# A two-layer decoder trunk on one core: projections of unnormed tokens, with the norm weights in the weight splits and the token factors at the results

## The chip, the cores and the metric

The kernel runs on one core of a Trainium2 chip. The metric is device time in microseconds (us), from one launch of the whole program; lower is better. It was run three times.

## The reference, cut to what matters

Two layers work on x, 512 tokens of 1024 values, in fp32. Each layer has a mixer, a cross attention into 256 memory tokens and a mixture of experts (MoE); each sub-layer is fed by an RMS norm with its own weight vector.

```python
def rms_norm(x, g):
    y = x * rsqrt(mean(x * x, axis=-1, keepdims=True) + EPS)
    return y * g

for layer in range(2):
    h = rms_norm(x, norm_mix[layer])
    x = x + (fox_rglru_mixer(h, ...) if layer % 2 == 0 else spatial_gating_mixer(h, ...))
    x = x + memory_cross_attention(rms_norm(x, norm_cross[layer]), rms_norm(mem, norm_mem[layer]), ...)
    x = x + hierarchical_moe(rms_norm(x, norm_ffn[layer]), ...)

# fox_rglru_mixer:       q, k, v, f_logit, xb, gb = split(h @ w_in); forgetting attention on q, k, v;
#                        a gated linear recurrence on xb with gate gelu(gb); concat, @ w_out
# spatial_gating_mixer:  u, v = split(gelu(h @ w_in + b_in)); v = rms_norm(v);
#                        mixed = causal 128x128 position mixing of v per group + b_s; (u * mixed) @ w_out
# memory_cross_attention: q = rms_norm(h @ wq); k, v = split(mem_n @ wkv); k = rms_norm(k); softmax; @ wo
```

A projection of normed tokens, h @ w, is r * (x @ (g * w)), with one factor r for each token and one weight g for each row of w. The norms of q and k inside a projection's result hardly feel r at all: only their EPS does.

## The kernel before

All engines run one program written by hand, in five instruction streams that meet in semaphores. Work stands in each stream in a fixed order, and an engine that waits holds up everything behind it.

**Dense projections.** Every fp32 product is made of three products of rounded parts (fp32r): weight high by activation high (`wh`, `ah`), weight low by activation high (`wl`, `ah`), weight high by activation low (`wh`, `al`). A weight matrix is cut into chunks of 512 columns (`("in", l, c)`, `("cin", l, c)`, `("cout", l, c)`, `("kv", l, c)`, `("xq", l, c)` and so on), a chunk into steps of 128 rows (8, or 16 for `cout`). For each step ScalarE (ACT) rounds 128x512 weights from the ring into `wh` (`split_hi`, L524), VectorE (DVE) makes the rest `wl` (`split_lo`, L533), and TensorE (PE) issues 12 products (L657, or L654 where the result is wanted transposed, `flip`), 6 where the rows are the 256 memory tokens. `wh` and `wl` have three places (STAGE = 3), so a split waits until PE has used the step three before. `between={k: work}` puts other work into a stream ahead of step k; `lead` makes the first three steps go token tile by token tile, so that they can begin before all four tiles are there; `split_next` makes the first three splits of the next chunk.

**Results.** PSUM's eight banks are two halves of four. Each chunk, turn or small product is a "round" on one half; `begin` on PE waits until every earlier round on that half has been reported by `took` on DVE or ACT. `HALF` and `names` in `round_plan` say which half and in which order. After `begin` a chunk fills the half.

**Norms.** For each of the kinds mix, cross and mem: ACT squares and sums a tile of tokens (`tile_square`, L1344), GpSimd (POOL) adds EPS and takes the power -1/2 (`norm_power`, L2447, L2448), DVE writes x * r * g into a buffer `nat` (`scale`, L1791), PE turns it into PSUM with 8 transposes of 128x128 (`norm_T`, L700), ACT rounds it (`tile_hi`, L1361), DVE makes the rest (`tile_lo`, L1812). The weight rows g come in broadcast loads of 512 KB (`load_gain`).

**Order of the stages.** Layer 0: norm; chunks in 0 to in 4 (q, k, xb, v, gb) with the forget logits `thin_f` (L719) ahead of step 3 of in 0, the turns of q and k, and the maxima products (`tops`) between the steps of in 3 and in 4; two gate products (L876); scores and values (L843 to L858); out 0, out 1. Layer 1: norm; cin 0 to 3 (v), cin 4 to 7 (u), cout 0 with the spatial products (L910) between its steps, cout 1. In both: the turns of the memory tokens, kv 0 to 2, the turns of the cross tokens, xq 0, xq 1, kv 3, attention, xo, routing, then 16 pairs of experts. Some filler products keep PE at work while it would wait: `idle_turns` (L689) and `idle_products` (L683). At the end of a MoE the last pair is added by `last_adds` on DVE (L2330).

## Time and profile before

| | |
|---|---|
| median of 3 runs | 1936.49 us (1935.87 to 1937.17) |
| the profiled execution, its own time | 1935.72 us |
| its span, from the first to the last instruction | 1934.0 us |
| PE busy | 1888.2 us, 98% |
| DVE, ACT, POOL busy | 41%, 28%, 5% |
| mean granted clock of TensorE | 0.996 |

The profiled execution is one more run; its span leaves 1.7 us around it. "Busy" of PE counts the filler products too, and a pipelined matmul's end is modelled, so 98% is not 98% useful work. The granted clock is a share of full speed: 1.00 is 2.4 GHz, 0.50 is 1.2 GHz. A wait in a row of the timeline stands in brackets, with the instruction that ended it.

### The profile page before, as it was taken

Reading aid. Unit: us, or ns where it says so; the run is one execution under the profiler, and the core shown is the slowest. Engines: PE = TensorE matmul, PEld = TensorE weight load, DVE = VectorE, ACT = ScalarE, POOL = GpSimd, SP = SyncE. Lnnn points to the kernel's source line nnn. Section 1 sums busy time; section 2 is a strip of 40 time slices with the busy share of each in tenths; the row PEclk is TensorE's granted clock in tenths of the full one; section 3 lists DMA queues with packets and bytes.
Section 4 is the critical chain, followed back from the end, with each engine's and each line's share of the span. In section 5 each row is a group of like instructions: output and inputs, shape, how many; then the busy total and the mean of one; then the engine's idle time right before and its main releaser. Section 6 shows DMA issues by size and latency. Waiting matters only on the chain.

```text
span 1934.0 us, 22569 instructions
## 1 busy us (share of the span) xinstructions
PE 1888.2 (98%) x9316; PEld 1198.4 (62%) x9316; DVE 786.9 (41%) x1184; ACT 543.8 (28%) x1008; POOL 94.7 (5%) x121
## 2 busy tenths in 40 slices
PE   8999999999999999999999999999999999999998
PEld 7875777676444544444588887777674444544443
DVE  4465565535222322223433356455371322323223
ACT  4426353533111111111344333335351111111110
POOL 2200010000000000000100022000000000000000
PEclk9999999999999999999999999999999999999999
DMA  6210342135999999999733312332138999999997
GB/s 242 88 66 22 110 152 87 44 112 197 406 420 415 421 418 418 419 416 423 275 104 118 107 64 87 114 127 87 47 131 363 418 416 420 421 418 420 421 415 288
DMA packets 96409, 490.06 MB, mean 253 GB/s; under 512 B 7824, under 2 KB 7888, under 8 KB 47024
## 3 DMA queue, kind: packets, MB, share of 16 engines
q1 hardware_dynamic: 93552, 479.75, 62.5%
q0 software_dynamic: 2176, 7.76, 1.2%
q8 instruction: 78, 1.28, 0.3%
q10 hardware_dynamic: 576, 1.05, 0.1%
q14 instruction: 27, 0.22, 0.0%
HBM read 486.44 MB, written 2.10 MB: 253 GB/s over the span
## 4 chain that ended last, share of the span: by engine, by line
PE 86%; DVE 6%; ACT 4%; DMA 2%; issue 2%; POOL 1%; SPq 0%; POOLq 0%; DVEq 0%; ACTq 0%
PE ps L657 24%; PE ps L1064 22%; PE ps L1088 11%; PE ps L1029 6%; PE ps L654 6%; PE ps L1050 5%; PE ps L981 1%; ACT wh L524 1%; PE ps L700 1%; PE ps L858 1%; PE ps L962 1%; DVE wl L533 1%; PE ps L1043 1%; DMA ring<-in_moe_w_down 1%; DMA ring<-in_c_w_in 1%
## 5 line engine op out<-in xcount | busy, mean ns | idle before, releaser
L533 DVE TENSOR_TENSOR wl<-ring,wh 128x512 fp32r<-128x512 f32 x280 | 199.9, 724 | 334.7 <-ACT wh L524 333.5
L524 ACT ACTIVATE wh<-ring 128x512 fp32r<-128x512 f32 x280 | 174.1, 629 | 366.2 <-PE ps L657 285.5
L1064 PE MATMUL ps<-ring,xg 128*64 128x512 f32 x1248 | 276.0, 594 | 0.3
L657 PE MATMUL ps<-wh,ah 128*128 128x512 f32 x544 | 215.8, 397 | 4.9 <-issue 2.3
L657 PE MATMUL ps<-wh,al 128*128 128x512 f32 x544 | 212.1, 390 | 0.0
L657 PE MATMUL ps<-wl,ah 128*128 128x512 f32 x544 | 211.8, 389 | 0.0
L2260 DVE SCALAR_TENSOR_TENSOR hh<-ps,wcol,sg 128x512 f32<-128x512 f32 x32 | 36.9, 1152 | 387.9 <-PE ps L1064 387.9
L1064 PEld LDWEIGHTS ps<-ring,xg 128*64 128x64 f32 x1248 | 87.7, 137 | 172.7 <-issue 171.9
L2281 DVE TENSOR_TENSOR x<-ps,x 128x1024 f32<-128x1024 f32 x120 | 144.1, 1222 | 87.7 <-PE ps L1050 83.9
L1064 PE MATMUL ps<-slot,xg 128*64 128x512 f32 x800 | 177.8, 594 | 0.0
L1667 ACT ACTIVATE xg<-ps,grow 128x256 f32<-128x256 f32 x128 | 53.6, 471 | 283.2 <-PE ps L1029 264.6
L1088 PE MATMUL ps<-ring,hT 128*64 128x512 f32 x576 | 128.6, 595 | 0.0
L1064 PEld LDWEIGHTS ps<-slot,xg 128*64 128x64 f32 x800 | 56.3, 137 | 111.2 <-issue 111.2
L1029 PE MATMUL ps<-oh,xnh 128*128 128x256 f32 x480 | 122.2, 293 | 0.0
L657 PEld LDWEIGHTS ps<-wh,ah 128*128 128x128 f32 x544 | 102.2, 188 | 28.8 <-issue 3.3
L1029 PEld LDWEIGHTS ps<-oh,xnh 128*128 128x128 f32 x480 | 90.1, 188 | 47.1 <-issue 47.1
L2278 DVE TENSOR_TENSOR yl<-ps,yh 128x512 fp32r<-128x512 f32 x64 | 41.4, 686 | 185.9 <-ACT yh L1650 185.9
L1029 PE MATMUL ps<-oh,xnl 128*128 128x256 f32 x480 | 116.2, 281 | 0.0
L657 PEld LDWEIGHTS ps<-wh,al 128*128 128x128 f32 x544 | 102.1, 188 | 21.7
L657 PEld LDWEIGHTS ps<-wl,ah 128*128 128x128 f32 x544 | 102.2, 188 | 20.7 <-issue 0.5
L1650 ACT ACTIVATE yh<-ps 128x512 fp32r<-128x512 f32 x64 | 35.0, 596 | 254.7 <-PE ps L1088 246.5
L1050 PE MATMUL ps<-yh,selT 128*128 128x512 f32 x240 | 97.5, 406 | 0.0
(312 smaller groups left out, 2622.2 us busy)
## 6 DMA issues: line engine op xcount, KB each, us to landing
ring<-in_moe_w_gate SPq DMA_DIRECT2D x80, 1024.0 KB, 10.2
ring<-in_moe_w_up SPq DMA_DIRECT2D x76, 1024.0 KB, 10.9
ring<-in_moe_w_down SPq DMA_DIRECT2D x76, 1024.0 KB, 9.2
slot<-in_moe_w_up SPq DMA_DIRECT2D x52, 1024.0 KB, 10.1
slot<-in_moe_w_down SPq DMA_DIRECT2D x52, 1024.0 KB, 9.4
slot<-in_moe_w_gate SPq DMA_DIRECT2D x48, 1024.0 KB, 10.6
ring<-in_x_wkv SPq DMA_DIRECT2D x16, 1024.0 KB, 5.0
ring<-in_c_w_in SPq DMA_DIRECT2D x16, 1024.0 KB, 5.4
```

The costliest lines, as they stand in the source:

```text
L524: act.activation(wh[:, t % STAGE, :], ring[:, SLOT[unit], 512 * s:512 * (s + 1)], ACT.Copy).then_inc(wh_ready, 1)
L533: dve.tensor_tensor(wl[:, t % STAGE, :], ring[:, SLOT[unit], 512 * s:512 * (s + 1)], wh[:, t % STAGE, :].bitcast(F32), ALU.subtract).then_ ...
L654: mm = pe.matmul(ps[:, b + m, 0:T], w[:, (t0 + k) % STAGE, m * P:(m + 1) * P], a[:, k, :], **flags)
L657: mm = pe.matmul(ps[:, b + m, :], a[:, (k + k0) % steps, m * P:(m + 1) * P], w[:, (t0 + k) % STAGE, :], **flags)
L1029: mm = pe.matmul(ps[:, bank, kk * 256:(kk + 1) * 256], a[:, m, k * P:(k + 1) * P], oh[:, b % 2, m, :], start=(m == 0 and i == 0), stop=(m ...
L1050: mm = pe.matmul(ps[:, bank + half, :], selT[:, q % 2, m * P:(m + 1) * P], a[:, 512 * half:512 * (half + 1)], start=(i == 0), stop=(i == 1))
L1064: mm = pe.matmul(ps[p * SLOTS:(p + 1) * SLOTS, bank, :], xg[:, b % 2, k, r * P + p * SLOTS:r * P + (p + 1) * SLOTS], w(p)[:, k % 4, :], st ...
L1088: mm = pe.matmul(ps[p * SLOTS:(p + 1) * SLOTS, Y + half, :], hT[:, k, p * SLOTS:(p + 1) * SLOTS], w(p)[:, k % 2, 512 * half:512 * (half + 1)],
L1667: ins = act.activation(xg[:, b % 2, k, :], ps[:, bank, kk * 256:(kk + 1) * 256], ACT.Copy, scale=grow[:, l, k:k + 1])
L2260: return dve.scalar_tensor_tensor(out=hh[:, :].rearrange("p (k c) -> p k c", k=KF), in0=by_row(ps[:, UP, :]), scalar=wcol[:, 0:1], in1=by_ ...
L2278: return dve.tensor_tensor(yl[:, part], ps[:, Y + half, :], yh[:, part].bitcast(F32), ALU.subtract)
L2281: return dve.tensor_tensor(x[:, m, :], ps[:, bank:bank + 2, :].rearrange("p a n -> p (a n)"), x[:, m, :], ALU.add)
```

## The change

Tokens are no longer multiplied by r and g before they are turned. PE turns x and mem themselves; `nat`, its scales and the broadcast loads of g go. Three small loads on ACT's queue bring all g of the kinds mix, cross and mem, PE turns them once, and DVE copies them to `gcols`, a column of 128 for each step. The splits of in, cin, kv and xq take that column as a scale: ACT's copy has a scale operand, and DVE's subtraction becomes multiply and subtract (`scalar_tensor_tensor`). The factor r is applied where each result leaves PSUM: as a column where tokens are rows, and as a row over all partitions, `rrow`, where they are columns. PE makes `rrow` with four products of a broadcast column with the identity (`norm_row`), once in `thin_f` and once ahead of step 7 of cin 3, as a round of its own. The EPS of the q and k norms is scaled by the variance (`epsn`).

Work that moves with it:
- the squares of the mix norm go from before the turns into in 0 and cin 0 (ahead of ACT's splits 4, 5 and 6);
- `thin_f` goes from step 3 to step 6 of in 0, `f_inputs`, `f_terms` and `f_sums` go into in 1, ahead of its steps 1, 2 and 3;
- xb goes from an ACT copy to four DVE multiplies behind kTr in `k_out`, and the second k copy goes from DVE to ACT;
- gb and u are multiplied by `rrow` on DVE and then put through Gelu on ACT, from SBUF instead of PSUM; the last four multiplies of u stand between the first four `gated` steps;
- the cross tokens' turns 0, 1 and 2 go into kv 1 and kv 2, their high and low parts with them; turn 3 into the lead of xq 0;
- the memory tokens' turns of layer 1 go from step 14 of cout 0 to step 6 of cout 1;
- the first weight unit of in 0 is loaded right behind the first tile of x; the turns of the mix tokens of layer 0 go into the lead of in 0;
- the banks of the last mixes and of the turns change, so that the first two turns of layer 1 can begin while the last adds run.

```diff
-LAST_MIX = ((6, 7, 0, 1), (2, 5, 3, 4))
+LAST_MIX = ((6, 7, 5, 1), (2, 4, 3, 0))
...
-            names += [("cin", l, c) for c in range(4)] + [("cin", l, c) for c in range(4, 8)]
-            names += [("mix", l, 0), ("cout", l, 0)] + [("nmem", l, m) for m in range(MM)] + [("cout", l, 1)]
-            half.update({("mix", l, 0): 0, ("cout", l, 0): 1, ("nmem", l, 0): 0, ("nmem", l, 1): 0, ("cout", l, 1): 0})
-        names += [("kv", l, c) for c in range(3)]
-        names += [("ncross", l, m) for m in range(TM)] + [("xq", l, 0), ("xkT", l, 0), ("xkT", l, 1), ("xq", l, 1)]
+            names += [("cin", l, c) for c in range(4)] + [("rrow", l, 0)] + [("cin", l, c) for c in range(4, 8)]
+            names += [("mix", l, 0), ("cout", l, 0), ("cout", l, 1)] + [("nmem", l, m) for m in range(MM)]
+            half.update({("rrow", l, 0): 0, ("cin", l, 4): 0})
+            half.update({("mix", l, 0): 0, ("cout", l, 0): 1, ("nmem", l, 0): 1, ("nmem", l, 1): 1, ("cout", l, 1): 0})
+        names += [("kv", l, 0), ("ncross", l, 0), ("kv", l, 1), ("ncross", l, 1), ("kv", l, 2), ("ncross", l, 2), ("ncross", l, 3)]
+        names += [("xq", l, 0), ("xkT", l, 0), ("xkT", l, 1), ("xq", l, 1)]
         names += [("kv", l, 3)]
         half.update({("nmix", l, m): l for m in range(TM)})
-        half.update({("ncross", l, m): 1 for m in range(TM)})
+        half.update({("ncross", l, m): 0 if m == 1 else 1 for m in range(TM)})
...
+                g = gain_of_step(t)
                 if s == 0:
                     act.wait_ge(ring_full[SLOT[unit]], 16 * NTH_LOAD[unit])
                 after(act, w_used, t - STAGE + 1)
                 act.activation(wh[:, t % STAGE, :], ring[:, SLOT[unit], 512 * s:512 * (s + 1)],
-                               ACT.Copy).then_inc(wh_ready, 1)
+                               ACT.Copy, **({} if g is None else dict(scale=g))).then_inc(wh_ready, 1)
...
-                dve.tensor_tensor(wl[:, t % STAGE, :], ring[:, SLOT[unit], 512 * s:512 * (s + 1)],
-                                  wh[:, t % STAGE, :].bitcast(F32), ALU.subtract).then_inc(wl_ready, 1)
+                g = gain_of_step(t)
+                if g is None:
+                    dve.tensor_tensor(wl[:, t % STAGE, :], ring[:, SLOT[unit], 512 * s:512 * (s + 1)],
+                                      wh[:, t % STAGE, :].bitcast(F32), ALU.subtract).then_inc(wl_ready, 1)
+                else:
+                    dve.scalar_tensor_tensor(out=wl[:, t % STAGE, :], in0=ring[:, SLOT[unit], 512 * s:512 * (s + 1)], scalar=g,
+                                             in1=wh[:, t % STAGE, :].bitcast(F32), op0=ALU.mult, op1=ALU.subtract)\
+                       .then_inc(wl_ready, 1)
             return max(pos, upto)
...
-                    sp.wait_ge(nat_ready, nats_upto("cross", l))
+                    sp.wait_ge(S["rec_ready"], 4)
                 elif SLOT[unit] == RING + 3:
                     sp.wait_ge(S["half_squares"], 2 * TM * (l + 1))
                     sp.wait_ge(S["small_lo"], l + 2)
...
                     after(pe, taken[HALF[name]], NTH[name] - (1 if kind == "ncross" or m else 0))
                     b = first_bank(name)
-                    nats[0] += 1
-                    pe.wait_ge(nat_ready, nats[0])
+                    src = mem if kind == "nmem" else x
                     for k in range(KD):
+                        if k == 0 and kind == "nmem":
+                            pe.wait_ge(S["mem_loaded"], 16 * (l + 1))
+                        if k == 0 and kind == "ncross":
+                            pe.wait_ge(res_added, TM * 2 * l + m + 1)
+                        if k == 0 and kind == "nmix" and l == 0:
+                            pe.wait_ge(x_loaded[m], 16)
+                        if k == 0 and kind == "nmix" and l and m == 0:
+                            pe.wait_ge(S["half_out"], TM * (l - 1) + 2)
+                        if k == (0 if m else KD // 2) and kind == "nmix" and l:
+                            pe.wait_ge(S["y_added"], TM * (PAIRS * l - 1) + m + 1)
                         mm = pe.transpose(ps[:, b + k // 4, (k % 4) * P:(k % 4 + 1) * P],
-                                          nat[:, m % 2, k * P:(k + 1) * P], ident[:, :])
...
+            def norm_row(l, bank):
+
+                pe.wait_ge(norm_rstd, nats_upto("mix", l))
+                for m in range(TM):
+                    mm = pe.matmul(ps[:, bank, m * P:(m + 1) * P], rnorm[:, 0, m:m + 1].to_broadcast([P, P]), ident[:, :],
+                                   start=True, stop=True)
+                return mm
...
-                mm.then_inc(acc_done, 1)
+                        pe.matmul(ps[:, b, 0:T], thin_w[:, c:c + P], a[:, k, :],
+                                  start=(k == 0 and i == 0), stop=(k == KD - 1 and i == 2))
+                norm_row(l, b + 1).then_inc(acc_done, 1)
...
-                dense("in", l, 0, ah, al, lead=tile_ready("nmix", l), between={3: lambda: thin_f(l)})
+                dense("in", l, 0, ah, al, lead=tile_ready("nmix", l, {(0, 1): 1, (0, 2): 2, (1, 1): 3}),
+                      between={6: lambda: thin_f(l)})
                 dense("in", l, 1, ah, al, between={7: c_turn})
...
             def gmlp(l):
-                for c in range(4):
-                    dense("cin", l, c, ah, al, lead=tile_ready("nmix", l) if c == 0 else None)
+                pe.wait_ge(S["y_added"], TM * PAIRS * l)
+                dense("cin", l, 0, ah, al, lead=tile_ready("nmix", l, {(1, 0): 2, (2, 0): 3}))
+                for c in range(1, 3):
+                    dense("cin", l, c, ah, al)
+
+                def row():
+                    b = begin(("rrow", l, 0))
+                    norm_row(l, b).then_inc(acc_done, 1)
+
+                dense("cin", l, 3, ah, al, between={7: row})
                 for c in range(4, 8):
...
                 idle_products(4 * HALF["cout", l, 0], 14)
                 dense("cout", l, 0, gh, gl, ready=lambda k: pe.wait_ge(S["gt_lo"], k + 1), between=between)
-                dense("cout", l, 1, gh, gl)
+                dense("cout", l, 1, gh, gl, between={6: lambda: norm_T("nmem", l, range(MM))})
 
             def cross(l):
-                for c in range(3):
-                    dense("kv", l, c, mh, ml, rows=MM)
+                nc = lambda m: lambda: norm_T("ncross", l, [m])
+                dense("kv", l, 0, mh, ml, rows=MM)
+                dense("kv", l, 1, mh, ml, rows=MM, between={2: nc(0)})
+                dense("kv", l, 2, mh, ml, rows=MM, between={2: nc(1), 6: nc(2)})
                 n0 = (2 if l == 0 else 6)
...
 
             for l in range(LAYERS):
                 if l == 0:
-                    idle_turns(6, 16)
+                    idle_turns(6, 4)
+                    pe.wait_ge(S["gains_loaded"], 48)
+                    pe.transpose(ps[:, 7, 0:3 * LAYERS * KD], gstage[:, :], ident[0:3 * LAYERS * KD, 0:3 * LAYERS * KD])\
+                      .then_inc(S["gains_turned"], 1)
+                    norm_T("nmix", l, [0])
+                    idle_turns(6, 20)
+                else:
                     norm_T("nmix", l, range(2))
-                    idle_turns(6, 4)
-                    norm_T("nmix", l, [2])
-                    idle_turns(6, 8)
-                    norm_T("nmix", l, [3])
-                else:
-                    pe.wait_ge(S["half_out"], TM * (l - 1) + 1)
-                    idle_turns(LAST_MIX[0][0], 4)
-                    norm_T("nmix", l, range(2))
-                    idle_turns(2, 10)
+                    pe.wait_ge(S["half_out"], TM * l)
+                    idle_turns(LAST_MIX[0][3], 8)
...
-                split(("in", l), 0, {7: f_terms})
-                split(("in", l), 1, {3: squares0})
+                def k_copy():
+                    b = round_done(act, ("kT", l, 0))
+                    act.wait_ge(S["k_rounded"], 1)
+                    for g in range(A_PAIRS):
+                        ins = act.activation(kT[:, g, :], ps[:, b + g, :], ACT.Copy, scale=kg[:, :])
+                    ins.then_inc(S["k_copied"], 1)
+
+                split(("in", l), 0, {4: lambda: square(0), 5: lambda: square(1), 6: lambda: [square(m) for m in (2, 3)]})
+                split(("in", l), 1, {2: f_terms, 3: squares0})
                 split(("in", l), 2, {0: c_keys, 3: lambda: head_squares(("in", l, 1), TM, A_DIM)})
-                split(("in", l), 3, {0: q_out, 3: lambda: copy_out(("in", l, 2), lambda m: xbT[:, m, :], range(4))})
-                split(("in", l), 4, {3: lambda: copy_out(("in", l, 3), lambda m: v0[:, m, :], range(TM))})
+                split(("in", l), 3, {0: q_out, 3: k_copy})
+                split(("in", l), 4, {3: lambda: copy_out(("in", l, 3), lambda m: v0[:, m, :], range(TM), "mix")})
                 b = round_done(act, ("mT", l, 0))
...
                 split_next()
-                copy_out(("in", l, 4), lambda m: gbT[:, m, :], range(4), ACT.Gelu_apprx_tanh)
+                for m in range(4):
+                    act.wait_ge(S["gb_scaled"], m + 1)
...
+                    dve.tensor_scalar(kTr[:, :, :], ps[:, b:b + A_PAIRS, :], kg[:, :], None, ALU.mult).then_inc(S["k_rounded"], 1)
+                    b = round_done(dve, ("in", l, 2))
+                    for m in range(4):
+                        ins = dve.tensor_tensor(xbT[:, m, :], ps[:, b + m, :], rrow[:, :], ALU.mult)
+                    ins.then_inc(took(("in", l, 2)), 1)
+                    wait_taken(dve, ("in", l, 2))
+                    dve.wait_ge(S["k_copied"], 1)
+                    dve.engine_nop().then_inc(took(("kT", l, 0)), 1)
 
...
                     return lambda: [step() for step in steps]
 
-                split(("in", l), 0, {6: f_inputs, 8: f_sums})
-                split(("in", l), 1, {3: lambda: head_means(("in", l, 0), *args),
+                split(("in", l), 0)
+                split(("in", l), 1, {1: f_inputs, 3: both(f_sums, lambda: head_means(("in", l, 0), *args)),
                                      6: lambda: head_scales(("in", l, 0), *args, lambda m: qn[:, m, :])})
                 split(("in", l), 2, {3: lambda: head_means(("in", l, 1), *args),
                                      6: lambda: head_scales(("in", l, 1), *args, lambda m: kn[:, m, :])})
...
+                b = round_done(dve, ("in", l, 4))
+                for m in range(4):
+                    dve.tensor_tensor(gbT[:, m, :], ps[:, b + m, :], rrow[:, :], ALU.mult).then_inc(S["gb_scaled"], 1)
+                dve.wait_ge(S["gb_scaled"], 4)
+                dve.engine_nop().then_inc(took(("in", l, 4)), 1)
...
 
-                split(("cin", l), 5)
+                def u_scale(c, m):
+                    def run():
+                        b = round_done(dve, ("cin", l, c))
+                        n = 4 * (c - 4) + m
+                        dve.tensor_tensor(uT[:, n, :], ps[:, b + m, :], rrow[:, :], ALU.mult).then_inc(S["u_scaled"], 1)
+                        if m == 3:
+                            dve.wait_ge(S["u_scaled"], n + 1)
+                            dve.engine_nop().then_inc(took(("cin", l, c)), 1)
+                    return run
+
+                between = {3 + m: u_scale(4, m) for m in range(4)}
+                split(("cin", l), 5, between)
                 v_scale(0)()
-                split(("cin", l), 6, {4: v_scale(1)})
+                between = {3 + m: u_scale(5, m) for m in range(4)}
+                between[1] = v_scale(1)
+                split(("cin", l), 6, between)
                 v_scale(2)()
-                between = {3 + m: (lambda m=m: scale("nmem", l, m, mem)) for m in range(MM)}
+                between = {3 + m: u_scale(6, m) for m in range(4)}
                 between[1] = v_scale(3)
                 split(("cin", l), 7, between)
                 split_next()
                 dve.wait_ge(S["bs_loaded"], 16)
...
                 between = {kt: gated(kt) for kt in range(4, 16)}
-                between[3] = gated(0, 1, 2, 3)
+                for m in range(4):
+                    u_scale(7, m)()
+                    gated(m)()
                 split(("cout", l), 0, between)
-                for m in range(MM):
-                    tile_lo(("nmem", l, m), mh, ml, m, KD)
```

## Rows read from the trace of the kernel before

**Rows 1.** The page: busy time by engine, and the chain that ended last.
```profile
PE 1888.2 (98%) x9316; PEld 1198.4 (62%) x9316; DVE 786.9 (41%) x1184; ACT 543.8 (28%) x1008; POOL 94.7 (5%) x121
...
PE 86%; DVE 6%; ACT 4%; DMA 2%; issue 2%; POOL 1%; SPq 0%; POOLq 0%; DVEq 0%; ACTq 0%
```

**Rows 2.** Busy time in six stretches: stretch, length, engines, granted clock, DMA share, GB/s.
```profile
12.00:17.00 5.00, 4.97 (x23) 4.60 (x24) 4.50 (x4) 4.05 (x8) 3.89 (x8) 0.50 1.05 387
...
46.10:68.40 22.30, 22.30 (x101) 18.22 (x100) 10.39 (x16) 7.08 (x13) 6.22 (x2) 1.00 0.30 95
...
263.00:287.30 24.30, 23.58 (x100) 18.17 (x99) 18.30 (x27) 11.85 (x21) 4.28 (x4) 1.00 0.54 182
...
287.30:302.00 14.70, 12.42 (x68) 9.71 (x66) 8.57 (x8) 6.82 (x9) 0.00 (x0) 1.00 0.13 51
...
942.00:944.00 2.00, 0.00 (x0) 0.00 (x0) 1.96 (x5) 1.82 (x5) 1.29 (x4) 1.00 1.05 394
...
946.00:948.00 2.00, 2.00 (x11) 2.00 (x10) 0.43 (x1) 0.81 (x1) 1.65 (x3) 0.50 0.06 22
```

**Rows 3.** Timeline and chain, start of layer 0: start, length, engine, line, instructions.
```profile
1.72 6.61 DMA x<-in_x
...
3.48 3.62 PE L689 MATMUL ps<-ident 128*128 128x128 f32 x16 [3.48 <-POOLq L2431]
...
8.38 1.09 PE L700 MATMUL ps<-ident,nat 128*128 128x128 f32 x8 [1.28 <-DVE nat L1791]
...
14.78 1.66 ACT L524 ACTIVATE wh<-ring 128x512 fp32r<-128x512 f32 x3
...
18.45 0.48 PE L657 MATMUL ps<-wh,ah 128*128 128x512 f32 x1
...
26.73 0.62 PE L719 MATMUL ps<-ah,thin_w 128*128 128x512 f32 x2
```

**Rows 4.** Timeline, from in 2 to in 3 of layer 0.
```profile
88.82 2.45 ACT L1428 ACTIVATE qT<-ps,qkg 128x512 f32<-128x512 f32 x4
...
93.18 2.00 ACT L1398 ACTIVATE xbT<-ps 128x512 f32<-128x512 f32 x4
...
94.08 2.35 DVE L1885 TENSOR_SCALAR kTr<-ps,qkg 128x2048 fp32r<-128x2048 f32 x1
...
95.24 0.50 PE L657 MATMUL ps<-wh,ah 128*128 128x512 f32 x1 [1.55 <-ACT xbT L1398]
```

**Rows 5.** Timeline and chain, start of layer 1.
```profile
940.23 3.68 DVE L2330 TENSOR_TENSOR x<-ps,x 128x512 f32<-128x512 f32 x6 [0.34 <-PE ps L1196]
...
945.38 3.48 PE L700 MATMUL ps<-ident,nat 128*128 128x128 f32 x16 [3.38 <-DVE nat L1791]
...
960.76 79.20 PE ps L657 x348
```

**Rows 6.** Timeline, from cin 7 to cout 0, and the memory tokens' turns.
```profile
1128.38 0.69 DVE L533 TENSOR_TENSOR wl<-ring,wh 128x512 fp32r<-128x512 f32 x1 [2.03 <-ACT wh L524]
...
1130.75 0.75 DVE L2055 SCALAR_TENSOR_TENSOR gt<-ps,small,bs 128x512 f32<-128x512 f32 x1 [1.68 <-ACT uT L1398]
...
1131.01 3.46 PE L683 MATMUL ps<-identr 128*128 128x512 f32 x14
...
1134.90 0.47 PE L657 MATMUL ps<-wh,gh 128*128 128x512 f32 x1 [0.43 <-POOL gl L2499]
...
1142.52 0.75 DVE L2055 SCALAR_TENSOR_TENSOR gt<-ps,small,bs 128x512 f32<-128x512 f32 x1 [1.63 <-PE ps L910]
...
1187.04 1.97 PE L700 MATMUL ps<-ident,nat 128*128 128x128 f32 x16 [1.63 <-DVEq L2061]
```

**Rows 7.** Timeline and chain: prices of work that the change adds or moves.
```profile
56.49 2.48 DVE L1832 TENSOR_TENSOR qn<-ps,rstd 128x512 f32<-128x512 f32 x4 [0.87 <-POOL rstd L2440]
...
228.98 2.47 DVE L1845 TENSOR_TENSOR x<-ps,x 128x512 f32<-128x512 f32 x4
...
1140.70 1.80 PE ps L910 x16
```

257 lines of the change are left out of this document (130 added, 127 removed).

## The prediction

> **What bounds the kernel now.** I read the page first. PE is busy for 98% of the span and carries 86% of the chain that ended last [rows 1], so only what shortens PE's own stream, or a place where it waits, can move the time. The products, three to each weight step and tile, stay as they are. Then I asked for busy time by stretch [rows 2], which shows where PE waits: not at all in in 1 (46.1 to 68.4), 0.7 us of 24.3 in kv 1 and kv 2, 2.3 us of 14.7 at the lead of xq 0, and at the starts of both layers. The timeline at each of these places shows what ended the wait [rows 3, 4, 5, 6]. The granted clock is half at 12 to 17 and at 946 to 948, in both cases after PE had had little or nothing to do [rows 2].
>
> All sums below are against the profiled execution's own 1935.72 us (span 1934.0, 1.7 around it). The median of the runs shown is 0.8 above it.
>
> **Start of layer 0.** Before: the first tile of x must be squared, scaled and turned; the first dense product is at 18.45, and the lead's 36 products end at 26.73, where thin_f starts [rows 3]. Tile 1 of x has landed at 1.72 + 6.61 = 8.33, after 1.5 MB. After: the first weight unit (1 MB, behind 0.5 MB of x) lands then instead, and tiles 1, 2 and 3 follow some 1.4 us apart: 9.7, 11.1, 12.4. Three rounded weights take 1.66 [rows 3], the rest 0.7 behind each, so products begin at about 10.0. PE then does in turn 0.7 of products, tile 1's turn (0.9), 0.7, tile 2's turn, 0.7; tile 1's low part is ready at 13.9; with tile 3's turn and the remaining products the lead ends at 21.1. That is 5.6 less than 26.7. Bounds: 6.0 if the loads are a little faster; 2.2 if PE runs at half clock until about 13.7, where three turns and products cost double (+3.4). I take 5.0. **-5.0 (-6.0 to -2.2).**
> On the clock the row shows: 16 turns ran from 3.48 for 3.62 us, 0.23 each, and the next 8, at 8.38, took 1.09, 0.13 each [rows 3]. So turns alone had brought the clock up. The Trainium skill (TensorE: Matmul & The Clock Gate, Part 4: PE-mode transpose) says that turns don't count as work for the clock gate; by that rule this term would be near -2.2 and not -5.0. The rows speak against it here; it is the second rival.
>
> **norm_row.** Four products of 128 columns in fp32. Eight such products (L910, two records each) take 1.80 [rows 7], so 0.9, on PE's own path, once in each layer. **+1.8.**
>
> **The forget gate moves into in 1.** thin_f costs the same at step 6. But f_inputs gains a copy and a multiply (1.4) and starts only behind it; exponentials and logarithm, f_sums and the squares of q follow on ACT and DVE, and splits wait behind them. Counted from in 1's start, the scaling of q (at 56.49, 10.4 after in 1's start at about 46.1 [rows 2, 7]) comes 3.6 later; split 6 behind it is then ready at 17.4 where PE wants it at 16.5. Before, PE never waited in in 1 [rows 2]. **+0.9 (0 to +1.5).**
>
> **k_out.** PE begins in 3 when the half holding xb is free. Before, ACT copies xb at 93.18, 2.00 for four, and PE goes on at 95.24 after waiting 1.55 [rows 4]. After, DVE does kTr first (94.08, 2.35) and then four multiplies from PSUM; four such operations take 2.47 [rows 7]. So 96.4 + 2.5 = 98.9. PE waits 5.2 instead of 1.55. Behind PE, nothing can hide it: in 3 and in 4 are PE's own pace. **+3.65.** The second k copy goes to ACT (about 2.45, as L1428 [rows 4]) and ends when the xb multiplies do; it costs nothing while that stays so, at most 0.3 otherwise.
> The clock: 3.4 us of waiting at the start of layer 1 [rows 5] were followed by half clock in 946 to 948 [rows 2], lasting 3.4 us in the trace. A wait of 5.2 should do the same. Half clock over 3.4 us of work costs 1.7. **+1.7 (0 to +3.4).**
>
> **gb.** DVE multiplies while ACT loads its table for Gelu; ACT sets this place. **0**, at most +0.7.
>
> **Cross attention, both layers.** Three turns move in front, between steps of kv 1 and kv 2, where DVE has lost two scales and PE gets slack; turn 3 stays in the lead. What goes is PE's waiting: 0.7 in kv 1 and kv 2 and 2.3 at the lead [rows 2], and some 0.25 at each of about three restarts. The turns themselves cost the same. **-3.8 each (-4.4 to -2.5), -7.6.** ACT's copy with a scale column takes 0.61 against 0.50 without (2.45 and 2.00 for four [rows 4]); in kv 0 ACT has a square ahead of each of four splits and sets the pace, so +0.4 a layer; in leads and restarts +0.3 in all. Elsewhere the PE work of a step (2.7) hides it. DVE's fused subtraction is read at 0.75 or less against 0.69 [rows 6], hidden likewise. **+1.1 (0 to +1.6).**
>
> **Start of layer 1.** Before: last adds from 940.23, six in 3.68; then squares, powers and scales; turns at 945.38 after 3.38 of waiting, 3.48 for two tiles at half clock; the even stream starts at 960.76 [rows 5]. After: tile 0's turn at 941.4, when PE's last mix ends, tile 1's at 942.3, ACT rounds at once. DVE makes tile 0's low part when its adds end, 943.9, so products start at 945.3 and go on nearly unbroken: 36 products (8.2), two turns (1.8), 0.4 of waits: 955.65. **-5.1 (-5.5 to -4.0).** The norm weights' load that went shared the queues with cin's first unit: **-0.2.** The squares now lie beside products.
>
> **rrow in cin 3.** It is a round of its own on the half that cin 4 needs. DVE reports it only after split_next, whose third split waits for cin 3's last step: a rounding of 0.6 (1.66 for three [rows 3]), a rest of 0.69 [rows 6], a copy of 0.62 (2.47 for four [rows 7]) and some 0.3 of passing on, so PE waits 2.2 between cin 3 and cin 4, which it did not before. **+2.2 (+2.0 to +3.9, the latter with half clock).** Behind that copy stand the last v parts and the next split, ready 0.3 before PE wants them.
>
> **Start of cout 0.** This is the costliest term. Before, ACT empties cin 7's half and DVE goes on behind it at 1130.75, PE runs 14 filler products from 1131.01, and the first step starts at 1134.90 [rows 6]. After, DVE starts u's last multiplies when its split ends (1129.07) and places two of `gated`'s operations (0.75 + 0.70) behind each. The half is free after the fourth multiply: 1129.1 + 4 x 0.65 + 3 x 1.5 (two operations with their hand-over) = 1136.3. Then come the 14 fillers (3.46): first step at 1139.8. Later work can't catch up: DVE's fifth `gated` waits for PE's spatial products behind step 1 (1142.52, after 1.63 of waiting [rows 6]) and the stage runs at DVE's and ACT's pace from there. **+4.9 (+4.0 to +6.5).** PE has waited 5.2 us, so again half clock: **+1.7 (0 to +3.4).**
> The memory turns leave cout 0, where PE waits 1.63 for the bank and then turns for 1.97 [rows 6], for cout 1, where PE has no slack. Steps 14 and 15 then wait for their splits and save only about 1.2 of the 3.6: **+0.65 (0 to +1.0).**
>
> **The sum.** -5.0 + 1.8 + 0.9 + 3.65 + 1.7 - 7.6 + 1.1 - 5.1 - 0.2 + 2.2 + 4.9 + 1.7 + 0.65 = +0.7. On 1935.72 this gives 1936.4, and with the 0.8 of the median **1937.2**. The MoE stages are untouched; their loads start as much earlier or later as PE's stream does.
>
> **Rivals.**
> First, the clock holds in both long waits (-3.4) and the gaps close whole (-1.0 at the start, -1.2 in cross): 1931.6. For it: in two of three places PE works hard right before the wait. Against it: the row at 946 to 948 after 3.4 of waiting.
> Second, slower: the clock comes back late. Turns and fillers don't bring it up at the start of layer 0 (+2.8), and it stays low twice as long after both waits (+3.4): 1943.4. In 12 to 17 the clock stayed at half although PE was busy for 4.97 of 5.00 [rows 2]. It decides from some 3 us more of half clock on.
> Third, the cross turns don't close their gap, because kv 2 can't begin before tile 0's low part is made on DVE: +7.6, 1944.8. By my count DVE is through 1.3 us before PE asks.
>
> **Numbers.** Forecast 0.50 (its own range 1934 to 1940.5), first rival 0.24, second 0.20, third 0.06. About 0.2% (3.9 us) is what a measurement of this kernel can tell from no change. The forecast spills a little over either edge: faster 0.24, same 0.49, slower 0.27. The range 1930 to 1944 takes in the first two rivals.
>
> **What would show it.** First product near 10 and thin_f's step near 29; PE waiting 5 us before in 3 and before cout 0's fillers, with half clock behind each; 2.2 before cin 4; layer 1's even stream starting 5 us sooner against the last adds; no wait in xq 0's lead. The prediction is wrong if DVE frees the halves in another order than I read, if the first weight unit lands much after 8.3, or if the clock acts otherwise.

## The result, and the profile after

The changed kernel takes 1945.52 us (median of 5, 1942.51 to 1946.47) against 1935.87 (1934.19 to 1937.17) for the one before, on the same chip: ratio 1.0049, 95% interval 1.0038 to 1.006. It is slower by 9.65 us; the forecast was 1937.2, with 1930 to 1944 as its range. The profiled execution has a span of 1943.8, against 1934.0.

The page of the changed kernel (rows 1 are the same lines of before):

```profile
PE 1890.3 (97%) x9323; PEld 1201.5 (62%) x9323; DVE 790.8 (41%) x1192; ACT 562.4 (29%) x1008; POOL 88.4 (5%) x122
...
PE 89%; DVE 5%; ACT 3%; issue 2%; POOL 0%; DMA 0%; POOLq 0%; ACTq 0%; DVEq 0%
...
L558 DVE SCALAR_TENSOR_TENSOR wl<-ring,gcols,wh 128x512 fp32r<-128x512 f32 x200 | 148.3, 750 | 217.3 <-ACT wh L544 216.0
...
L544 ACT ACTIVATE wh<-ring,gcols 128x512 fp32r<-128x512 f32 x200 | 142.1, 720 | 217.4 <-PE ps L684 166.4
```

PE has 2.1 us more of busy time in a span that is 9.8 longer. So 7.7 us of the difference are time in which PE did nothing (work at half clock counts as busy), and the places have to be found one by one. The two splits cost 750 and 720 ns with a weight column, hidden behind PE except at restarts.

Timeline of the changed kernel, start of layer 0 (its lines answer to rows 3):

```profile
1.72 0.51 ACTq L1791 DMA_DIRECT2D gstage<-in_norm_mem  x1
...
3.48 1.11 PE L714 MATMUL ps<-ident 128*128 128x128 f32 x4 [3.48 <-POOLq L2498]
...
8.16 0.34 PE L1351 MATMUL ps<-ident,gstage 48*128 48x48 f32 x1 [3.56 <-DMA gstage<-in_norm_mem]
...
8.43 1.97 PE L734 MATMUL ps<-ident,x 128*128 128x128 f32 x8
...
10.19 4.46 PE L714 MATMUL ps<-ident 128*128 128x128 f32 x20
10.44 1.02 ACT L1413 ACTIVATE ah<-ps 128x1024 fp32r<-128x1024 f32 x1 [6.90 <-PE ps L734]
11.36 1.94 ACT L544 ACTIVATE wh<-ring,gcols 128x512 fp32r<-128x512 f32 x3
11.57 1.23 DVE L1851 TENSOR_TENSOR al<-ps,ah 128x1024 fp32r<-128x1024 f32 x1 [2.82 <-ACT ah L1413]
12.71 2.07 DVE L558 SCALAR_TENSOR_TENSOR wl<-ring,gcols,wh 128x512 fp32r<-128x512 f32 x3
...
26.20 0.50 PE L684 MATMUL ps<-wh,ah 128*128 128x512 f32 x1 [0.31 <-DVE wl L558]
```

PE stands still until the third small load of norm weights has landed (1.72 + 6.4 = 8.12), then turns tile 0 and runs 20 idle turns at 0.22 each. The first rest is ready near 13.4 (a third of the 2.07 behind 12.71), but the idle turns go on until 14.3. The first product is at 14.32 (forecast 10.0), and the lead ends at 26.20, only 0.5 earlier than before.

The same kernel where in 3 begins (rows 4), and busy time by stretch there, with PE's granted clock in the third column from the end:

```profile
96.50 2.35 DVE L1928 TENSOR_SCALAR kTr<-ps,qkg 128x2048 fp32r<-128x2048 f32 x1
98.77 2.47 DVE L1931 TENSOR_TENSOR xbT<-ps,rrow 128x512 f32<-128x512 f32 x4
...
101.29 0.79 PE L684 MATMUL ps<-wh,ah 128*128 128x512 f32 x1 [5.44 <-DVE xbT L1931]
```
```profile
100.00:107.00 7.00, 5.71 (x14) 4.49 (x15) 1.24 (x3) 1.55 (x4) 0.00 (x0) 0.52 0.00 0
```

This is the step as forecast: kTr, then the multiplies, and PE waits 5.44. The half clock lasts 6.8 us, not 3.4; it begins near 99.8, so its first 1.5 us lie under the wait and 5.3 us of products run at half pace.

The same kernel at the start of layer 1 (rows 5) and before cin 4:

```profile
945.92 1.93 PE L734 MATMUL ps<-ident,x 128*128 128x128 f32 x16
...
947.68 0.38 PE L714 MATMUL ps<-ident 128*128 128x128 f32 x2
948.46 2.35 DVE L1851 TENSOR_TENSOR al<-ps,ah 128x1024 fp32r<-128x1024 f32 x2
...
950.64 0.88 PE L714 MATMUL ps<-ident 128*128 128x128 f32 x6 [2.57 <-issue]
951.27 0.48 PE L684 MATMUL ps<-wh,ah 128*128 128x512 f32 x1
...
962.35 0.50 PE L684 MATMUL ps<-wh,ah 128*128 128x512 f32 x1 [0.23 <-DVE wl L558]
...
1043.25 0.75 DVE L558 SCALAR_TENSOR_TENSOR wl<-ring,gcols,wh 128x512 fp32r<-128x512 f32 x1 [2.90 <-ACT wh L544]
1043.92 0.68 DVE L2081 COPY rrow<-ps 128x512 f32<-128x512 f32 x1
...
1044.65 0.50 PE L681 MATMUL ps<-ah,wh 128*128 128x512 f32 x1 [2.20 <-DVE rrow L2081]
```

Tile 0's low part is ready at 949.7, but PE is in a pause of 2.57 us that nothing in the trace ends ("issue"), and runs six idle turns behind it; the first product is at 951.27. Before cin 4 the wait is the forecast 2.20.

The same kernel at the start of cout 0 (rows 6), and the stretch over it:

```profile
1134.93 0.68 DVE L2101 TENSOR_TENSOR uT<-ps,rrow 128x512 f32<-128x512 f32 x1
...
1136.30 0.69 DVE L2135 TENSOR_TENSOR gt<-gt,uT 128x512 f32<-128x512 f32 x1
...
1138.29 1.33 DVE L2135 TENSOR_TENSOR gt<-gt,uT 128x512 f32<-128x512 f32 x1
...
1142.09 0.68 DVE L2101 TENSOR_TENSOR uT<-ps,rrow 128x512 f32<-128x512 f32 x1
...
1142.88 5.71 PE L708 MATMUL ps<-identr 128*128 128x512 f32 x14 [5.69 <-DVEq L2104]
...
1148.43 0.40 PE L684 MATMUL ps<-wh,gh 128*128 128x512 f32 x1
```
```profile
1140.00:1150.00 10.00, 7.12 (x21) 5.68 (x22) 4.53 (x6) 2.93 (x5) 3.82 (x3) 0.66 0.00 0
```

Between u's first and last multiply lie 7.2 us; PE waits 5.69, and the fillers then take 5.71 at half clock instead of the 3.46 of before.

Set against the prediction's terms, the two timelines give this ledger. Each point is the start of an instruction of PE that both kernels have. "Shift" is how much later it comes than before; the measured column is the step in it.

| stretch, and its end before / after | shift at its end | forecast | measured |
|---|---|---|---|
| start of layer 0 (26.73 / 26.20) | -0.5 | -5.0 | -0.5 |
| norm_row and forget gate (68.25 / 70.41) | +2.15 | +1.8 | +2.7 |
| wait before in 3 (95.24 / 101.29) | +6.05 | +3.65 | +3.9 |
| half clock behind it (124.33 / 132.86) | +8.5 | +1.7 | +2.45 |
| cross of layer 0 (312.06 / 316.80) | +4.75 | -3.25 | -3.8 |
| to the last mix of layer 0 (937.65 / 942.12) | +4.5 | 0 | -0.3 |
| start of layer 1 (960.76 / 962.35) | +1.6 | -5.3 | -2.9 |
| norm_row and wait before cin 4 (1039.79 / 1044.65) | +4.85 | +3.1 | +3.3 |
| half clock behind it (1127.52 / 1133.46) | +5.9 | 0 | +1.1 |
| to the first product of cout 0 (1134.90 / 1148.43) | +13.5 | +6.6 | +7.6 |
| cout 1 and cross of layer 1 (1299.88 / 1309.06) | +9.2 | -2.6 | -4.3 |
| rest (1934.0 / 1943.8) | +9.8 | 0 | +0.6 |

The cross terms are -3.8 with 0.55 of the +1.1 for ACT; cout 1 holds the +0.65.

### The profile page after: what moved, and what is told of

Same layout as the page of the kernel before. It is cut to its first block, busy times and chain, and to the rows that moved or that the text cites. A ratio compares the mean times of both kernels' runs of the same rounds, so it can differ in the third digit from the quotient of the medians.

```text
span 1943.8 us, 22604 instructions
## 1 busy us (share of the span) xinstructions
PE 1890.3 (97%) x9323; PEld 1201.5 (62%) x9323; DVE 790.8 (41%) x1192; ACT 562.4 (29%) x1008; POOL 88.4 (5%) x122
## 3 DMA queue, kind: packets, MB, share of 16 engines
q8 instruction: 78, 1.28, 0.3%
## 4 chain that ended last, share of the span: by engine, by line
PE 89%; DVE 5%; ACT 3%; issue 2%; POOL 0%; DMA 0%; POOLq 0%; ACTq 0%; DVEq 0%
PE ps L684 24%; PE ps L1116 23%; PE ps L1140 11%; PE ps L681 7%; PE ps L1081 6%; PE ps L1102 6%; PE ps L1033 1%; ACT wh L544 1%; PE ps L901 1%; PE ps L1014 1%; PE ps L734 1%; PE ps L1095 1%; DVE wl L558 1%; PE ps L1130 1%; PE ps L1123 1%
## 5 line engine op out<-in xcount | busy, mean ns | idle before, releaser
L558 DVE SCALAR_TENSOR_TENSOR wl<-ring,gcols,wh 128x512 fp32r<-128x512 f32 x200 | 148.3, 750 | 217.3 <-ACT wh L544 216.0
L544 ACT ACTIVATE wh<-ring,gcols 128x512 fp32r<-128x512 f32 x200 | 142.1, 720 | 217.4 <-PE ps L684 166.4
L555 DVE TENSOR_TENSOR wl<-ring,wh 128x512 fp32r<-128x512 f32 x80 | 62.9, 791 | 114.1 <-ACT wh L544 113.9
```

Source lines behind the costliest of these rows:

```text
L544: act.activation(wh[:, t % STAGE, :], ring[:, SLOT[unit], 512 * s:512 * (s + 1)], ACT.Copy, **({} if g is None else dict(scale=g))).then_i ...
L555: dve.tensor_tensor(wl[:, t % STAGE, :], ring[:, SLOT[unit], 512 * s:512 * (s + 1)], wh[:, t % STAGE, :].bitcast(F32), ALU.subtract).then_ ...
L558: dve.scalar_tensor_tensor(out=wl[:, t % STAGE, :], in0=ring[:, SLOT[unit], 512 * s:512 * (s + 1)], scalar=g, in1=wh[:, t % STAGE, :].bitc ...
```

## The experiments

Every one is an edit of the changed kernel, so its time is to be held against 1945.5. But they ran on three chips, where the kernel before took 1935.08 (the runs of u's multiplies, the row's copy, xb early and the first start), 1935.43 (no turns, cross turns back, four edits together) and 1934.78 (the third start and all edits), against the 1935.87 beside the changed kernel. So each difference to 1945.5 is followed, in brackets, by the one that results when each of the two kernels is held against the kernel before as measured beside it. Differences of 2 us and less aren't clear of the noise by the time alone; there the trace decides.

**u's multiplies first.**

```diff
                 for m in range(4):
                     u_scale(7, m)()
+                for m in range(4):
                     gated(m)()
```

> DVE does the four multiplies of u's last column group together, and only then the first four gated tiles; nothing else differs from the changed kernel. Theory A (the half of the projection's last round is freed late because each multiply stands behind a gated tile, and those go round two buffers through ACT and POOL): the fourth multiply ends near 1137.4 instead of 1142.8, the fillers start at once behind the spatial products (1137.2) and run in 3.5 us at full clock, the first product of cout 0 is near 1141.0 instead of 1148.4, and the time falls by 7.5 us against the changed kernel, to about 1938.0. Rival B (cout 0 is paced by the gated tiles whatever the order: 0.74 + 0.69 on DVE, 0.63 on ACT, 1.27 on POOL, and two buffers): the first product comes no earlier than 1140.8, and the steps behind it wait for their tiles, so that 3 to 4 us of the gain are given back: about 1941.5. Rival C (the half clock stays although the wait is gone): 1939.7.

1938.23 us (1935.36 to 1941.06), ratio to before 1.0015 (1.0006 to 1.0024): 7.3 less (6.5). Timeline of this run:

```profile
1133.74 2.47 DVE L2101 TENSOR_TENSOR uT<-ps,rrow 128x512 f32<-128x512 f32 x4
...
1136.33 3.47 PE L708 MATMUL ps<-identr 128*128 128x512 f32 x14 [0.32 <-DVEq L2104]
...
1140.48 0.47 PE L684 MATMUL ps<-wh,gh 128*128 128x512 f32 x1 [0.69 <-POOL gl L2573]
```

The wait falls from 5.69 to 0.32, the fillers are back at 3.47, and cout 0 loses nothing later: at its last spatial products the run is as far ahead of the changed kernel (7.9) as at its start. Theory A: the order is the cause. Of its reason, the two buffers, no row shows a part: DVE never waits for one there.

**The row's copy first.**

```diff
-                split_next()
                 b = round_done(dve, ("rrow", l, 0))
                 dve.tensor_copy(rrow[:, :], ps[:, b, :]).then_inc(took(("rrow", l, 0)), 1)
+                split_next()
```

> DVE copies the factors' row ahead of the three splits of cin 4, not behind them; nothing else differs from the changed kernel. Theory A (the 2.20 us that PE waits before cin 4, and the half clock behind it, come from that copy standing behind a split that waits for cin 3's last step): the wait goes and with it the half clock (3.4 us of it, a loss of 1.6), while the wait of 0.4 that the kernel before had behind the v parts comes back: 3.4 us less than the changed kernel, about 1942.1. Rival B (the clock falls because of the row's eight small products and not of the wait): only 2.2 less, 1943.3. Rival C (DVE now waits for the row and its splits are late, so PE waits for them instead): no difference.

1941.74 us (1939.29 to 1942.93): 3.8 less (3.0). A row of its timeline, and its stretch over 1040 to 1060:

```profile
1049.53 0.50 PE L681 MATMUL ps<-ah,wh 128*128 128x512 f32 x1 [0.76 <-DVE wl L558]
```
```profile
1040.00:1060.00 20.00, 19.24 (x85) 1.00 0.27 79
```

There is no wait before cin 4, the granted clock is 1.00 (0.91 in the run above, which keeps the wait), and a later wait of 0.76 stands behind the v parts (0.39 in the kernel before). Theory A. B is out because the row's eight small products are still there and the clock holds, C because PE's wait is gone.

**xb's multiplies early, and in the middle.** The first run takes the four multiplies out of k_out into xb_out:

```diff
-                split(("in", l), 3, {3: k_out, 4: lambda: conv(0),
+                split(("in", l), 3, {0: xb_out, 3: k_out, 4: lambda: conv(0),
```

> DVE multiplies xb by the factors' row as soon as in 2 is done, ahead of in 3's first splits and of the rounding of k; nothing else differs from the changed kernel. Theory A (PE waits 5.4 us before in 3 for multiplies that stand behind the splits and the 2.35 us of k's rounding, and the half clock behind it costs 2.45): the half is free near 96.4, the first split is ready near 97.2, so PE starts in 3 at about 97.2 instead of 101.3, at full clock: 6.5 us less than the changed kernel, about 1939.0. Rival B (a wait of 1.4 still takes the clock down): 4.1 less, 1941.4. Rival C (k's rounding, 2.4 later, is now late for the row maxima in in 3's step 3): about half is given back there, 1942.

1940.73 us (1939.15 to 1943.09): 4.8 less (4.0). Timeline of this run:

```profile
97.30 0.47 PE L684 MATMUL ps<-wh,ah 128*128 128x512 f32 x1 [1.58 <-DVE wl L558]
...
113.38 0.56 PE L860 MATMUL ps<-kTr,qTr 64*128 64x384 f32 x4 [0.40 <-DVE nmax L1943]
...
119.11 0.56 PE L860 MATMUL ps<-kTr,qTr 64*128 64x512 f32 x4 [1.17 <-DVE nmax L1943]
```

PE starts where expected and the clock stays full, so 6.4 us are won at this place; that is theory A, and B is out. But 1.6 are given back: with PE earlier, DVE, which now has the multiplies, is late with the row maxima. None of the three theories had that; C named the neighbouring wait, for k's rounding, which didn't occur. The second run keeps the multiplies at step 3, ahead of k's rounding (`3: both(xb_out, k_out)`):

> One look. The changed kernel with xb's multiplies directly ahead of k's rounding, behind in 3's first splits. Theory A (DVE's order alone sets the wait, and a wait of 2.2 was enough for half clock before cin 4): PE starts in 3 near 99.0 instead of 101.3, after a wait of 3.1, with half clock behind it of 3.4 us or more. Rival B (the wait is now short enough for the clock to hold): full clock throughout, tops 2.3 + 2.4 sooner.

One execution, 1943.21 us:

```profile
97.99 0.79 PE L684 MATMUL ps<-wh,ah 128*128 128x512 f32 x1 [3.16 <-DVE xbT L1929]
```
```profile
100.00:105.00 5.00, 5.00 (x15) 3.90 (x14) 0.92 (x3) 3.15 (x5) 0.00 (x0) 0.58 0.00 0
```

The wait is 3.16, and half clock follows it, for 6.8 us again (0.87 granted in 90 to 100, 0.58 in 100 to 105): theory A. The half clock didn't get shorter when the wait went from 5.44 to 3.16; with 1.58, in the run before, it was gone.

**The start of layer 0, in three forms.** First, 16 turns and tile 0's turn ahead of the wait for the norm weights:

```diff
-                    idle_turns(6, 4)
+                    idle_turns(6, 16)
+                    norm_T("nmix", l, [0])
                     pe.wait_ge(S["gains_loaded"], 48)
...
-                    norm_T("nmix", l, [0])
-                    idle_turns(6, 20)
+                    idle_turns(6, 12)
```

> At the start of layer 0 PE runs 16 idle turns instead of 4, then turns the first tile of x, and only then waits for the norm weights and turns them, with 12 idle turns behind instead of 20; the loads are as they were. Theory A (PE's turns stood behind the third small load, which lands at 8.1, and PE was cold again by then, so that its first tile, 20 turns and the wait for the clock went until 14.3): the tile is turned by 8.3 at full pace, gcols are ready at 8.8, the first rounded weight and its rest by 10.2, and the first product comes at 10.5 instead of 14.3; the lead ends 3.5 to 4 us earlier and the time is about 1941.8. Rival B (the first weight unit of 1 MB lands only at 10 or later, and the tiles behind it): the first product at 12 or later and 1 to 2 us less, 1944. Rival C (turns don't bring the clock up; what had done so was the long row of 8 + 20 turns): the first products run at half pace and 1 us is gained at most.

1943.63 us (1941.34 to 1944.39): 1.9 less (1.1), near what rival B gave, but not for its reason. Timeline of this run, and its stretch at the start of layer 1:

```profile
6.95 1.92 PE L734 MATMUL ps<-ident,x 128*128 128x128 f32 x8
...
9.07 1.63 PE L714 MATMUL ps<-ident 128*128 128x128 f32 x12
...
12.07 0.47 PE L684 MATMUL ps<-wh,ah 128*128 128x512 f32 x1 [1.37 <-DVE wl L558]
...
947.66 0.44 PE L734 MATMUL ps<-ident,x 128*128 128x128 f32 x2 [2.20 <-issue]
```
```profile
945.00:950.00 5.00, 2.80 (x16) 0.80 0.51 193
```

Here PE waits for DVE's first rest, which stands behind the tile's low part, that behind the high part, that behind a turn at half pace. The lead ends at 23.85, 2.35 sooner than in the changed kernel. But at the start of layer 1 half clock follows the pause, which the changed kernel doesn't have, and from the last mix to the end of that lead this run loses 1.2 (18.90 against 17.66). So the time hides half of what the start won. Whether the load was late too, the second form shows: the mixing norm's weights get a semaphore and a turn of their own, and ACT and DVE split ahead of the tile.

> One look. As the run with 16 turns ahead, and besides the norm weights of the mixing norm get a semaphore and a turn of their own, ahead of the first tile's, the other two follow behind it, and at the start ACT and DVE split the first three weight steps ahead of the first tile. Theory A (the first weight unit of 1 MB has landed at 8.3 or before, and what held the first product to 12.07 there was the late gains and the tile's rounding ahead of the weights'): ACT's first rounding starts at 8.3, the first product follows the tile's high part at 11.3. Rival B (the first weight unit lands later than 9): ACT's first rounding starts when that load ends, and the trace names the load.

One execution, 1945.85 us:

```profile
8.18 1.28 ACT L544 ACT_TABLE_LOAD   x1 [8.18 <-DMA ring<-in_ab_w_in]
...
13.64 0.50 PE L684 MATMUL ps<-wh,ah 128*128 128x512 f32 x1 [2.61 <-DVE al L1860]
```

The first weight unit has landed at 8.18, so rival B is out; the prediction's 8.3 was right. Theory A's first product at 11.3 was not: ACT's first operation with data now pays for loading its table (1.28), and the tile is the late one, so the first product comes at 13.64. Splits first is the wrong order. The third form keeps tile first, turns it as early as x allows and takes the other norm weights out of the way:

```diff
+                    idle_turns(6, 6)
+                    pe.wait_ge(S["mix_loaded"], 16)
+                    pe.transpose(ps[:, 5, 0:LAYERS * KD], gstage[0:LAYERS * KD, :], ...)
+                    norm_T("nmix", l, [0])
+                    idle_turns(6, 14)
+                    pe.wait_ge(S["gains_loaded"], 32)
```

> Start of layer 0 only: PE runs 6 idle turns, turns the mixing norm's weights (8 KB, its own semaphore), then the first tile of x, then 14 idle turns and only then the other norm weights; ACT and DVE round the tile first and the weights behind it, as in the changed kernel. Theory A (the first unit lands near 8.2, as ACT's table load in the run with splits first shows, and what held the first product was the chain small loads, turn at half pace, high part, low part, rests): tile 0 is turned by 6.7, its low part is made by 9.0, the first rest is ready at 9.7, the first product comes near 9.9 instead of 14.3, and if the clock is up by then the lead ends 4 us sooner: about 1941.5. Rival B (PE's clock is not up until 12 or later, as the turns pause): the products run at half pace until then and 2 us are gained, 1943.5.

1941.6 us (1939.67 to 1943.4): 3.9 less (2.8). Timeline of this run:

```profile
5.17 1.97 PE L734 MATMUL ps<-ident,x 128*128 128x128 f32 x8
...
6.93 3.16 PE L714 MATMUL ps<-ident 128*128 128x128 f32 x14
...
10.34 0.47 PE L684 MATMUL ps<-wh,ah 128*128 128x512 f32 x1
...
22.20 0.50 PE L684 MATMUL ps<-wh,ah 128*128 128x512 f32 x1 [0.31 <-DVE wl L558]
```

First product at 10.34, at full pace, and the lead ends at 22.20, 4.0 sooner than in the changed kernel. Theory A: most of the gain that the prediction counted was there, behind the order of small things (22.20 against the 21.1 of the prediction).

**Start of layer 1.** Without the turns and their wait:

```diff
-                    pe.wait_ge(S["half_out"], TM * l)
-                    idle_turns(LAST_MIX[0][3], 8)
```

> The changed kernel without the eight idle turns at the start of layer 1 and without the wait for the first half's adds ahead of them. In the changed kernel two of them ran and then nothing for 2.57 us that no engine or load ended, then six more; the first product came 1.8 us after the first tile's low part was ready. Theory A (the pause belongs to PE's own instruction supply at this place of the program and not to the turns or the adds): the pause is still there and ends near where it did, so the time changes by less than 0.7 us. Rival B (the turns and their wait cost it): the first product follows the low part at once, 1.7 us less, about 1943.8. Rival C (the turns kept the clock up): half clock behind the pause, 1.5 us or more slower.

1943.76 us (1939.83 to 1945.69): 1.8 less (1.3). The row of the first product:

```profile
949.15 0.47 PE L684 MATMUL ps<-wh,ah 128*128 128x512 f32 x1 [2.09 <-DVE al L1849]
```

It follows the low part at once, 7.8 behind the first product of the last mix instead of 9.15, so 1.3 are won at this place, and the granted clock stays 1.00. That is B: the turns and their wait cost the time, and A's bound of 0.7 was wrong. No row of this run shows the pause. It may lie under the wait of 2.09 for the low part; that isn't shown. That the pause belongs to the program and not to the place, the next run tells:

> One look. The changed kernel with 12 more idle turns at the very start of PE's program (16 before the first tile and 20 behind it). The pause at the start of layer 1 stood behind the 16 turns of tiles 0 and 1 and two idle turns in the changed kernel, behind 14 turns of tiles where 4 turns more ran at the start of the program, and behind 13 where 5 more did. Theory A (the pause sits at a fixed number of instructions in PE's program): now 12 fewer, behind the sixth turn of the tiles, some 2 to 2.6 us long, no engine or load named. Rival B (it belongs to what PE does there): it stays behind the turns of the tiles.

```profile
944.82 0.82 PE L734 MATMUL ps<-ident,x 128*128 128x128 f32 x6
948.77 2.29 PE L734 MATMUL ps<-ident,x 128*128 128x128 f32 x10 [3.13 <-issue]
```

It sits behind the sixth turn, exactly as counted, and is 3.13 long (one execution, 1943.73 us). In the third start, with three instructions fewer ahead, it sits three further on; in the first, with four more, four sooner (behind 14 turns), and in the run with the splits first, with five more, five sooner (behind 13). What fills PE's instructions there, and why it is late, no row shows.

**The cross turns put back** behind kv 2 and into xq 0's lead, in both layers, with their banks and their high and low parts (an excerpt):

```diff
-                dense("kv", l, 1, mh, ml, rows=MM, between={2: nc(0)})
-                dense("kv", l, 2, mh, ml, rows=MM, between={2: nc(1), 6: nc(2)})
+                dense("kv", l, 1, mh, ml, rows=MM)
+                dense("kv", l, 2, mh, ml, rows=MM)
...
+                norm_T("ncross", l, range(2))
```

> The changed kernel with the turns of the cross tokens put back: tiles 0 and 1 behind kv 2, tiles 2 and 3 in the lead of xq 0, as in the kernel before, in both layers; token factors and norm weights stay where the change put them. Theory A (moving the turns is what took 3.7 us out of each layer): 7.4 slower than the changed kernel, about 1952.9. Rival B (the squares and scales that left DVE and ACT had closed the gap already, and the place of the turns matters little): at most 3 slower, 1948.5.

1953.4 us (1952.72 to 1955.12), ratio to before 1.0092: 7.9 slower than the changed kernel (8.3). Theory A.

**The edits together.** First the four of u, the row, xb early and the first form of the start:

> The four edits of the runs with u's multiplies first, the row's copy first, xb's multiplies early and the start with 16 turns ahead, together in the changed kernel. Theory A (the four places are independent stretches of PE's one stream, so their gains add): 7.3 + 3.8 + 4.8 + 1.9 = 17.8 less than the changed kernel's 1945.5, about 1927.7, which is 7 to 8 below the kernel before. Rival B (an earlier stream meets the expert weights' loads, which then end waits of PE in the expert stage, or the start of layer 1 takes part of it): at least 4 given back, 1932 or more.

1930.47 us (1928.84 to 1931.22), ratio to before 0.9969 (0.9959 to 0.998): 15.0 less (14.6). By the times this is 2.8 short of the sum, 17.8. But that sum counts four times that the kernel before, too, took 0.8 less beside these runs than beside the changed kernel. Held against it, the four runs won 6.5 + 3.0 + 4.0 + 1.1 = 14.6, and this one has 14.6. So the stretches are independent within the noise, as theory A has it, and B's 4 us are not there. At the start of layer 1 this run has half clock behind the pause (0.91 granted in 940 to 945), which costs 1.7:

```profile
945.00:950.00 5.00, 5.00 (x25) 0.75 0.01 3
```

Of that, 1.2 are already in the result of the first start. Then also the third form of the start, and no turns in layer 1:

> The changed kernel with u's multiplies first, the row's copy first, xb's multiplies early, the start of the run before, and without the eight idle turns and their wait at the start of layer 1. Theory A (independent stretches): 1930.5 as with the first four edits, less 1.8 for the turns, less 1.7 for the half clock that the run with four edits had at the start of layer 1, less 2 for the start: 1925, some 10 below the kernel before. Rival B (the half clock at the start of layer 1 stays, and the start gains nothing over 16 turns ahead): 1928.7.

1928.53 us (1928.09 to 1929.66), ratio 0.997 (0.9959 to 0.9982): 17.0 less than the changed kernel (15.9) and 6.3 less than the kernel before on that chip (1934.78). It beats both, and missed theory A by 3.5. Rival B's number (1928.7) is hit, but by luck: the trace has full granted clock from 935 to 960, so B's first half is out, and the lead's gain is there (-4.0), so the second is too. Its last mix of layer 1 comes 19.1 us sooner than in the changed kernel while its span, 1926.3, is only 17.5 shorter. The 1.6 between are in the last stores of the output: the final adds end 3.7 before the span's end in the changed kernel, 5.3 in this run and 4.4 in the kernel before. The remaining 2 aren't traced; 1.1 is what the kernel before took less on this chip.

## Why the prediction was wrong

The forecast of "about no change" (+0.7) failed by 9 us, and nearly all of it in what PE waits for and in filler turns, little in the products.

- **Start of layer 0: the step that failed most (+4.5).** "Three rounded weights take 1.66 [rows 3], the rest 0.7 behind each, so products begin at about 10.0." It counted from the 1 MB load alone. The load was on time (8.18, as the run with the splits first shows). The diff also holds `pe.wait_ge(S["gains_loaded"], 48)` ahead of tile 0's turn, on PE, which works in order; three loads of 8 KB land after 2.8, 4.0 and 6.4 us, the last at 8.12. Behind it stand a turn at half pace (1.97), high part, low part and rest, and then the last of 20 idle turns at half pace, on which the prediction has no word. Together they put the first product 4.3 late, at 14.32. The lead itself took 11.9 instead of 11.1. With PE waiting for one small load only, and the tile turned 3.3 sooner, the first product was at 10.34 and the lead ended at 22.20.
- **norm_row and the forget gate (+0.9).** 0.8 for the row, near the 0.9 forecast. PE waits 0.17 and 0.84 for splits, as forecast (0.9); the remaining 0.9 is spread and not traced.
- **k_out: right** (5.44 of waiting against 5.2). The half clock was counted as 3.4 us of work at 1.7 and took in 5.3 us of work at 2.45: +0.75.
- **Cross turns: right, and a little better.** -3.8 in layer 0, where -3.25 was forecast, and putting them back costs 7.9 for both. The third rival is out.
- **Start of layer 1 (+2.4).** The low part was ready at the forecast moment, 1.2 us behind the last adds. What was left out is eight idle turns and a pause among them: the first product stands 1.6 behind the low part. The lead then took 0.7 more than forecast (11.1 against 10.35), and of the 0.2 for the norm weights' load no row shows anything. In the kernel before PE waited 3.38 here [rows 5], and a pause could have lain under that wait; whether it did isn't shown. When a wait goes, ask what could lie under it.
- **rrow: the wait right (2.20), the clock behind it missed (+1.1).** It was kept as a bound and not in the sum.
- **cout 0 (+1.0).** "Half free at 1136.3" took two operations of `gated` for 1.5. DVE's multiply took 1.33 and 1.26 instead of 0.69 in two of the three pairs, while POOL worked on the tile before; so the half was free at 1142.8, which less the shift of 5.9 is 0.6 later than forecast. The fillers ran wholly at half clock and lost 2.25, where 1.7 was counted: 0.55 more. The mechanism was right: u's multiplies behind `gated` hold the half, and PE waited 5.69 where 5.2 was forecast.
- **cout 1 and cross of layer 1** came 1.7 better than forecast, the only large term on that side. Of it, 1.15 lie before kv 0: leaving cout 0 saved 1.4 (1.2 forecast), the memory turns cost 1.7 in cout 1, and the other 0.75 come from cout 1's pace, 2.72 for a step of 12 products where it was 2.77. Why it was faster no row shows. The remaining 0.6 lie in cross.
- **The rivals.** The first (clock holds) is out: it fell behind both waits that it spoke of. The second was near the time that came (1943.4), partly for its reason: at the start turns at half pace did cost, and the clock stayed low twice as long behind in 3 and before cout 0; but the longer half clock cost only 1.3 more there, not 3.4, and more than half of the miss is the small loads' chain, the idle turns and the pause, which it didn't name. That its number is near is partly luck.

On the clock at the start: in the run with 16 turns ahead, only turns had run when twelve of them took 1.63 at 9.07, 0.14 each, after 0.22 each from 3.48. The Trainium skill (TensorE: Matmul & The Clock Gate, Part 4: PE-mode transpose) says that turns don't count as work for the clock gate; by these rows they do bring PE to full pace here. In the changed kernel, with only 4 turns and then 3.56 of waiting ahead, the 20 turns from 10.19 stayed at 0.22. The granted clock can't decide it: it reads 1.00 throughout, at either pace.

## What to carry to other kernels

Moving a multiply to where the result leaves PSUM makes it part of the time in which the bank is taken: put it ahead of all that can wait on the same engine. Each of three such places (before in 3, cin 4 and cout 0) cost PE 2 to 6 us, then half clock on top, and each was mended by the order of a few lines, one of them with 1.6 us given back. The prediction had all three waits within 0.5 us, so the order could have been changed before anything ran. Work brought to the start of a kernel starts when its smallest, last load lands, so only that load's own users should wait for it. And before a wait is taken away, look for what else could be hidden under it.
